# Sums of squares added on VectorE, two products with ones for sixteen, and the last tiles of mix by halves on VectorE

## The reference, cut to what matters

```
h = rms_norm(x, norm_mix_g);  proj = h @ w_in              # first norm
x = x + (gates0 * (o_a @ w_o[:512]) + gates1 * (o_b @ w_o[512:])) @ w_merge   # mix, merge
h = rms_norm(x, norm_ffn_g)                                # second norm
x = x + (silu(conv(h @ w_gate)) * (h @ w_up)) @ w_down     # feed-forward
# rms_norm(t, g) = t * rsqrt(mean(t*t) + 1e-6) * g
```

## Time and profile before

| | |
|---|---|
| median of 3 runs | 3369.89 us (3364.22 to 3376.41) |
| profiled execution | 3384.76 us, its span 3382.9 us |
| TensorE busy, span | 3193.5 us, 94% |
| VectorE | 2035.6 us, 60% |
| ScalarE | 1068.7 us, 32% |
| GpSimd | 315.4 us, 9% |
| granted clock, mean | 0.971 |

### The profile page before, as it was taken

How to read it: one execution, slowest core, us unless ns; L and a number is a source line. 1 busy time by engine, 2 the same in 40 slices (tenths; PEclk the granted TensorE clock), 3 DMA queues, 4 the chain that set the end, 5 groups by cost and what they waited for, 6 DMA issues and landing times.

```text
span 3382.9 us, 52078 instructions
## 1 busy us (share of the span) xinstructions
PE 3193.5 (94%) x22004; PEld 2545.1 (75%) x22004; DVE 2035.6 (60%) x3235; ACT 1068.7 (32%) x1526; POOL 315.4 (9%) x307
## 2 busy tenths in 40 slices
PE   8999998788988888999999999999998999999999
PEld 7777786576766767778888888877746888778887
DVE  4665454577777775534544444448979987655445
ACT  5222334444444442221111111122153333433332
POOL 0222342000000000401000000000000000000000
PEclk9999999789999998999999999999999999999999
DMA  3342666234344433421111111111101222213222
GB/s 143 118 137 68 220 209 202 62 83 100 83 105 98 95 66 136 149 93 38 50 50 50 50 50 44 44 38 42 46 13 50 99 89 99 87 69 129 90 99 75
DMA packets 93527, 301.86 MB, mean 89 GB/s; under 512 B 10352, under 2 KB 38640, under 8 KB 70768
## 3 DMA queue, kind: packets, MB, share of 16 engines
q1 hardware_dynamic: 79104, 246.63, 23.5%
q0 software_dynamic: 14192, 51.91, 4.5%
HBM read 241.35 MB, written 57.15 MB: 88 GB/s over the span
## 4 chain that ended last, share of the span: by engine, by line
PE 78%; DVE 11%; issue 3%; ACT 3%; DMA 3%; POOL 2%; SPq 1%; DVEq 0%; ACTq 0%; POOLq 0%
PE ps L2414 24%; PE ps L308 20%; PE ps L503 6%; PE ps L1755 3%; PE ps L2239 2%; PE ps L2556 2%; PE ps L1766 1%; PE ps L2074 1%; PE ps L1778 1%; PE ps L475 1%; DVE Yh L2583 1%; PE ps L1423 1%; PE ps L1019 1%; DMA Dn<-nbs 1%; PE ps L2434 1%
## 5 line engine op out<-in xcount | busy, mean ns | idle before, releaser
L2414 PE MATMUL ps<-Hh,whi 128*128 128x512 f32 x1600 | 498.4, 393 | 0.0
L284 ACT ACTIVATE whi<-raw 128x2048 fp32r<-128x2048 f32 x139 | 265.7, 1911 | 638.3 <-PE ps L308 310.4
L288 DVE TENSOR_TENSOR wlo<-raw,whi 128x2048 fp32r<-128x2048 f32 x139 | 319.0, 2295 | 132.9 <-ACT whi L284 132.7
L2414 PEld LDWEIGHTS ps<-Hh,whi 128*128 128x128 f32 x1600 | 300.5, 188 | 68.0 <-issue 6.2
L2414 PE MATMUL ps<-Hh,wlo 128*128 128x512 f32 x800 | 311.6, 390 | 0.0
L2414 PE MATMUL ps<-aHh,whi 128*128 128x512 f32 x512 | 200.0, 391 | 3.6 <-DVE xT L2760 2.5
L308 PE MATMUL ps<-Hhi,wlo 128*128 128x512 f32 x656 | 202.2, 389 | 0.0
L308 PE MATMUL ps<-Hhi,whi 128*128 128x512 f32 x656 | 202.1, 389 | 0.0
L308 PE MATMUL ps<-Hlo,whi 128*128 128x512 f32 x656 | 202.1, 389 | 0.0
L2414 PE MATMUL ps<-aHh,wlo 128*128 128x512 f32 x512 | 199.4, 389 | 0.0
L2414 PE MATMUL ps<-aLh,whi 128*128 128x512 f32 x512 | 199.4, 389 | 0.0
(11 more groups left out here) (385 smaller groups left out, 6199.9 us busy)
## 6 DMA issues: line engine op xcount, KB each, us to landing
raw<-in_panels SPq DMA_DIRECT2D x139, 1024.0 KB, 4.7
rwf<-F POOLq DMA_DIRECT2D x16, 1280.0 KB, 6.8
L<-rwf SPq DMA_DIRECT2D x16, 1024.0 KB, 5.0
L<-rwf SPq DMA_DIRECT2D x64, 256.0 KB, 4.1
Dn<-nbs SPq DMA_DIRECT2D x128, 128.0 KB, 5.4
gts<-so POOLq DMA_DIRECT2D x16, 512.0 KB, 3.2
gl<-gts SPq DMA_DIRECT2D x32, 256.0 KB, 3.6
rwt<-so POOLq DMA_DIRECT2D x15, 512.0 KB, 3.0
```

Of the source, the lines that this page charges most:

```text
L284: e.activation(whi[i % 2][:, :], raw_of(i)[:, :], AF.Copy).then_inc(*a_hi.up(i))
L288: e.tensor_tensor(wlo[i % 2][:, :], raw_of(i)[:, :], whi[i % 2][:, :].bitcast(F32), OP.subtract).then_inc(*v_lo.up(i))
L2414: m = e.matmul(ap, W[wi][:, kc, n0:n0 + 128], mov[mi][:, kc, :], start=x == 0 and q == 0, stop=x == len(kcs) - 1 and q == 2)
```

## The change

Squares are now added on VectorE (`acc_dve`: chunk 1's to chunk 0's in `rs`, and so on), and TensorE multiplies only the result by ones (`norm_pe`). ACT's square waits for the addition two chunks before. In the first norm the two products stand in the first half of mla1, before chunk 4; the wait for bank tiles in `rw_pe` follows the turned ring. In the second norm the squares and additions of chunks 0 to 6 (additions 1 to 6) go into merge, those of chunk 7 behind it, and the two products before chunk 3 of `together_pe`, which now does two outputs; gate 1 becomes a group of its own behind it. In merge VectorE drains an odd tile before it makes the next panel's low part. In mix, the additions of tiles 6 and 7 are VectorE's, half by half; ACT makes their `Hhi` by halves, and VectorE `Hlo`, with tile 6's beside tile 7. The diff, without what only moves the first norm's start into helpers:

```diff
@@ -319,8 +319,10 @@
             aps.append(ap)
         return aps
 
-    def together_pe(e, outs, mov, r, sig):
+    def together_pe(e, outs, mov, r, sig, third=None):
         for kc in range(8):
+            if kc == 3 and third:
+                third()
             e.wait_ge(*v_h.by(r, "lo", kc))
             for aps, w, n0, n1, key in outs:
                 for q, (wi, mi) in enumerate(THREE):
@@ -332,21 +334,28 @@
 
     a_h, v_h, t_h = signals("a_h"), signals("v_h"), signals("t_h")
 
-    def rms_act(e, r, gname, tmp, rs, x_by, h_free):
-        e.wait_ge(*d_vec.by())
-        for kc in range(8):
-            e.wait_ge(*x_by(kc))
-            if kc >= 2:
-                e.wait_ge(*t_h.by(r, "sum", kc - 2))
-            e.activation(tmp[kc % 2], xT[:, kc, :], AF.Square).then_inc(*a_h.up(r, "sq", kc))
-            if kc == 0:
-                for w in h_free:
-                    e.wait_ge(*w)
-            e.activation(Hhi[:, kc, :], xT[:, kc, :], AF.Copy, scale=vec(gname, kc)).then_inc(*a_h.up(r, "hi", kc))
+    def square_act(e, r, kc, tmp):
+        if kc >= 2:
+            e.wait_ge(*v_h.by(r, "acc", max(kc - 2, 1)))
+        e.activation(tmp[kc % 2], xT[:, kc, :], AF.Square).then_inc(*a_h.up(r, "sq", kc))
+
+    def hi_act(e, r, kc, gname):
+        e.activation(Hhi[:, kc, :], xT[:, kc, :], AF.Copy, scale=vec(gname, kc)).then_inc(*a_h.up(r, "hi", kc))
+
+    def sqrt_act(e, r, rs):
         e.wait_ge(*v_h.by(r, "mean", 1))
         e.activation(rs, rs, AF.Sqrt).then_inc(*a_h.up(r, "sqrt"))
 
-    def rms_pe(e, r, tmp):
+    def acc_dve(e, r, kc, tmp, rs):
+
+        e.wait_ge(*a_h.by(r, "sq", kc))
+        if kc == 1:
+            e.tensor_tensor(rs, tmp[0], tmp[1], OP.add).then_inc(*v_h.up(r, "acc", kc))
+        else:
+            e.wait_ge(*v_h.by(r, "acc", kc - 1))
+            e.tensor_tensor(rs, rs, tmp[kc % 2], OP.add).then_inc(*v_h.up(r, "acc", kc))
+
+    def norm_pe(e, r, rs):
         aps = []
         for h in range(2):
             ap, waits = ring.take(("sum", r, h), (v_h, r, "mean", h))
@@ -354,25 +363,22 @@
                 e.wait_ge(*w)
             aps.append(ap)
         e.wait_ge(*d_cc.by())
-        for kc in range(8):
-            e.wait_ge(*a_h.by(r, "sq", kc))
-            for h in range(2):
-                m = e.matmul(aps[h], ones, tmp[kc % 2][:, hs(h)], start=kc == 0, stop=kc == 7)
-            m.then_inc(*t_h.up(r, "sum", kc))
-
-    def rms_dve(e, r, gname, rs, rs_free=()):
-        e.wait_ge(*d_vec.by())
-        for kc in range(8):
-            e.wait_ge(*a_h.by(r, "hi", kc))
-            e.scalar_tensor_tensor(out=Hlo[:, kc, :], in0=xT[:, kc, :], scalar=vec(gname, kc),
-                                   in1=Hhi[:, kc, :].bitcast(F32), op0=OP.mult,
-                                   op1=OP.subtract).then_inc(*v_h.up(r, "lo", kc))
-        e.wait_ge(*t_h.by(r, "sum", 7))
-        for w in rs_free:
-            e.wait_ge(*w)
+        e.wait_ge(*v_h.by(r, "acc", 7))
+        for h in range(2):
+            e.matmul(aps[h], ones, rs[:, hs(h)], start=True, stop=True).then_inc(*t_h.up(r, "sum", h))
+
+    def h_lo_dve(e, r, kc, gname):
+        e.wait_ge(*a_h.by(r, "hi", kc))
+        e.scalar_tensor_tensor(out=Hlo[:, kc, :], in0=xT[:, kc, :], scalar=vec(gname, kc), in1=Hhi[:, kc, :].bitcast(F32),
+                               op0=OP.mult, op1=OP.subtract).then_inc(*v_h.up(r, "lo", kc))
+
+    def means_dve(e, r, rs):
+        e.wait_ge(*t_h.by(r, "sum", 1))
         for h in range(2):
             e.tensor_scalar(rs[:, hs(h)], ring.bank("sum", r, h), 1.0 / KB, 1e-6, OP.mult,
                             OP.add).then_inc(*v_h.up(r, "mean", h))
+
+    def over_dve(e, r, rs):
         e.wait_ge(*a_h.by(r, "sqrt"))
         e.reciprocal(rs, rs).then_inc(*v_h.up(r, "rs"))
...
         e.wait_ge(*d_vec.by())
@@ -470,6 +457,8 @@
                 for kc in range(8):
                     if i == 0 and js[0] == 0:
                         e.wait_ge(*v_h.by(0, "lo", kc))
+                    if i == 1 and js[0] == 0 and kc == 4:
+                        norm_pe(e, 0, rs)
                     for j in js:
                         for q, (mi, wi) in enumerate(((0, 0), (0, 1), (1, 0))):
                             m = e.matmul(aps[j][:, 0:208], H2[mi][:, kc, 128 * j:128 * (j + 1)], W[wi][:, kc, :],
@@ -477,8 +466,6 @@
                         if kc == 7:
                             m.then_inc(*t_mla.up(i, j))
             last_use[p] = (t_mla, (i, 7))
-            if i == 0:
-                rms_pe(e, 0, tmp)
 
     def mla_act(e, i, j):
         e.wait_ge(*t_mla.by(i, j))
@@ -519,7 +506,7 @@
             if n0 == 0:
                 panel_pe(e, p)
             if ch < 2:
-                e.wait_ge(*a_mla.by("cols", 1, 6 * ch + 1))
+                e.wait_ge(*a_mla.by("cols", 1, 4 * ch + 3))
             front_pair(e, ("rw", ch), v_rw, "u", ch)
         half_group(e, [fring.bank("rw", ch, h) for h in range(2)], W, n0, n0 + M, half, t_rw, ch)
         if half:
@@ -1972,7 +1959,7 @@
             e.wait_ge(*(v_mx if h else g_mx).by("m", n - 1, h))
         e.dma_start(gl0[y % 2], gts[n][:, hs(h)]).then_inc(*d_g0.up(y))
         if y >= 3:
-            e.wait_ge(*g_mx.by(*seq[y - 3]))
+            e.wait_ge(*added(*seq[y - 3]))
         if y == 2:
             e.wait_ge(*t_mx.by("OT", 3, 0))
         e.dma_start(gl1[y % 3], gts[8 + n][:, hs(h)]).then_inc(*d_g1.up(y))
@@ -2124,8 +2111,13 @@
             if n == 4:
                 panel_act(e, WO + 4)
             e.wait_ge(*v_mx.by("OA", 3))
-            e.wait_ge(*g_mx.by(n, 1))
-            e.activation(Hhi[:, n, :], mix[n][:, :], AF.Copy).then_inc(*a_h.up("mix", "hi", n))
+            if n < 6:
+                e.wait_ge(*added(n, 1))
+                e.activation(Hhi[:, n, :], mix[n][:, :], AF.Copy).then_inc(*a_h.up("mix", "hi", n, 1))
+            else:
+                for h in range(2):
+                    e.wait_ge(*added(n, h))
+                    e.activation(Hhi[:, n, hs(h)], mix[n][:, hs(h)], AF.Copy).then_inc(*a_h.up("mix", "hi", n, h))
         panel_act(e, WO + 5)
 
     def mix_dve(e):
@@ -2144,21 +2136,35 @@
                 e.wait_ge(*d_g1.by(2 * n + h))
                 e.tensor_tensor(gl1[(2 * n + h) % 3], ring.bank("yb", n, h), gl1[(2 * n + h) % 3],
                                 OP.mult).then_inc(*v_mx.up("b", n, h))
-            if n:
+                if n >= 6:
+                    e.wait_ge(*(v_mx if h else g_mx).by("m", n, h))
+                    e.wait_ge(*v_mx.by("b", n, h))
+                    e.tensor_tensor(mix[n][:, hs(h)], mix[n][:, hs(h)], gl1[(2 * n + h) % 3], OP.add).then_inc(*v_mx.up("sum", n, h))
+                if n == 7:
+                    mixlo_dve(e, 6, h)
+            if 1 <= n < 7:
                 mixlo_dve(e, n - 1)
-        mixlo_dve(e, 7)
+        for h in range(2):
+            mixlo_dve(e, 7, h)
         panel_dve(e, WO + 5)
 
-    def mixlo_dve(e, n):
-        e.wait_ge(*a_h.by("mix", "hi", n))
-        e.tensor_tensor(Hlo[:, n, :], mix[n][:, :], Hhi[:, n, :].bitcast(F32), OP.subtract).then_inc(*v_h.up("mix", "lo", n))
+    def added(n, h):
+
+        return v_mx.by("sum", n, h) if n >= 6 else g_mx.by(n, h)
+
+    def mixlo_dve(e, n, h=None):
+        t = slice(0, S) if h is None else hs(h)
+        e.wait_ge(*a_h.by("mix", "hi", n, 1 if h is None else h))
+        m = e.tensor_tensor(Hlo[:, n, t], mix[n][:, t], Hhi[:, n, t].bitcast(F32), OP.subtract)
+        if h != 0:
+            m.then_inc(*v_h.up("mix", "lo", n))
 
     def mix_pool(e):
         for n in range(8):
             e.wait_ge(*a_mx.by("ya", n, 0))
             e.wait_ge(*d_g0.by(2 * n))
             e.tensor_tensor(mix[n][:, hs(0)], mix[n][:, hs(0)], gl0[0], OP.mult).then_inc(*g_mx.up("m", n, 0))
-            for h in range(2):
+            for h in range(2 if n < 6 else 0):
                 if h:
                     e.wait_ge(*v_mx.by("m", n, 1))
                 else:
@@ -2244,16 +2250,36 @@
 
     def merge_dve(e):
         for n in range(8):
-            if n % 2:
-                panels_after(panel_dve, e, UIX[f"mg{n // 2}"])
             e.wait_ge(*d_xs.by(n))
             for h in range(2):
                 e.wait_ge(*t_mg.by(n, h))
                 e.tensor_tensor(xT[:, n, hs(h)], ring.bank("mg", n, h), xs[n % 2][:, hs(h)], OP.add).then_inc(*v_mg.up(n, h))
+            if n in (1, 3, 5):
+                panels_after(panel_dve, e, UIX[f"mg{n // 2}"])
+            if 1 <= n < 7:
+                acc_dve(e, 1, n, tmp2, rs2)
+        h_lo_dve(e, 1, 0, "norm_ffn_g")
+        acc_dve(e, 1, 7, tmp2, rs2)
+        for kc in range(1, 8):
+            h_lo_dve(e, 1, kc, "norm_ffn_g")
+        means_dve(e, 1, rs2)
+        panels_after(panel_dve, e, UIX["mg3"])
+        over_dve(e, 1, rs2)
 
     def merge_act(e):
-        for n in range(1, 8, 2):
-            panels_after(panel_act, e, UIX[f"mg{n // 2}"])
+        for n in range(7):
+            e.wait_ge(*v_mg.by(n, 1))
+            square_act(e, 1, n, tmp2)
```

(57 more changed lines are left out.)

## The result

The changed kernel takes 3350.2 us in the median of 6 runs (3346.2 to 3356.4), beside 3371.93 (3364.22 to 3377.88) of the kernel before in 6. The ratio is 0.9937, 95% interval [0.9922, 0.9953]: 21 us shorter (16 to 26 by the interval), and 3350.7 had been forecast. The profiled execution took 3347.74.

What follows compares the result with a forecast made beforehand. The prediction took TensorE, with 78% of the chain of waits, to bound the kernel. First norm 5.9, mix 0 and second norm 13.3 summed to 19.2 us, so 3350.7 us against the median of 3369.89; its own range was 3344 to 3357.

Steps and rivals of the forecast that it cites:

- First norm, TensorE's side: First norm's products with ones: 11.7 us go, 1.7 stay; TensorE pauses 1.1 us for the last addition at 46.2.
- The root moves less: First norm's root and rst come only 2.7 us earlier; TensorE pauses 1.5 us more for tile copies.
- Latents: ACT's lat squares wait for rst instead of tile copies, so they and VectorE's latent work come 7.4 us earlier.
- ckv pause and half rate: TensorE's wait for ckv grows to 4.0 us; 7.4 passes, less 1.5 for a half-rate stretch: 5.9 us gained.
- Mix: Mix's last tiles, additions moved from POOL to VectorE: 0 us, bounds -1.5 (gain) and +2.8.
- Second norm: Between merge and feed-forward: 15.94 gone, 1.7 and 1.4 back, 0.5 pause gained: 13.3 us, bounds 11.5 and 15.
- Sum: Whole kernel: 5.9 + 0 + 13.3 = 19.2 us, giving 3350.7 against the median of 3369.89.
- Rival 1: Both norms' products pass in full, 23.4 us, plus the pause's 0.5: 3346 us; chance 0.14.
- Rival 2: Only the second norm pays, the first gives 2.7 or less: 16 us, 3354; chance 0.22 together with Rival 3.
- Rival 3: Additions don't overlap other work; first norm's TensorE gain is 0: 13 us, 3357; chance 0.22 together with Rival 2.
- Rival 4: Front part: TensorE pauses at each latent handover, then half rate; 20 stretches give 3380.7, 11 us slower; chance 0.04.

Runs made afterwards that it cites:

- no_mix: The changed kernel with mix's part undone; ratio to the kernel before 0.9934.
- warm_tail: The changed kernel plus 22 unread products issued while TensorE waits for mix's tile 6; ratio to the kernel before 0.9926.
- norm1_alone: The kernel before with only the first norm's part of the change; ratio to the kernel before 0.9954.
- early_norm: The changed kernel with the second norm's high and low parts of chunks 0 to 2 made during merge's last tile; ratio to the kernel before 0.9895.
- norm2_alone: The kernel before with only the second norm's part of the change; ratio to the kernel before 0.9958.
- mix_alone: The kernel before with only mix's part (tiles 6 and 7 added on VectorE, in halves); ratio to the kernel before 0.9994.
- root_late: The changed kernel with the first norm's two products before chunk 7 instead of chunk 4; ratio to the kernel before 0.9947.
- alone_products: The changed kernel with the first norm's two products between the two projections, where sixteen stood; ratio to the kernel before 0.9942.
- latents_first: The changed kernel with VectorE's rope of the shared key behind the ckv pieces instead of ahead; ratio to the kernel before 0.9903.

## Why the prediction was right

By its own steps:

- **First norm, TensorE's side.** Pause 1.1 foretold, 1.34 measured; last addition at 46.2, was 46.83. Additions take 1.31 us each (7.87 for six), not 1.26, and the projection began 0.5 later.
- **The root moves less.** 2.7 foretold, 53.32 - 51.39 = 1.9 measured. The tile copies' pause was 0.95, not 1.5.
- **Latents.** 7.4 earlier foretold, 74.44 - 67.80 = 6.6 measured: the same mechanism (ACT waited for rst, 1.85 us), shifted by the 0.8 us by which the root came later than I had it.
- **ckv pause and half rate.** A pause of 4.0 us was foretold, a gain of 7.4 at ckv, and one more stretch at half rate, so 5.9. Measured are 4.47, 7.1 counted from ACT's first copy, and 5.9 by the means at the front's end. That the last number is met to the tenth is luck, as two things behind ckv show that the prediction did not have. First, half rate: the kernel before has a stretch behind its pause of 2.44 us at 130.84. Changed, no_mix and warm_tail have one behind ckv and none behind that later pause, so in them it moved rather than came. norm1_alone and early_norm have both, as foretold (rows below). Second, TensorE waits for a DMA (`lw`) at 338 to 347 us, 5.29 and 4.92 us in the kernel before's profiles, 3.76 and 4.04 in norm2_alone and mix_alone, and 3.54 to 4.33 in the five with the change. Both scatter from profile to profile, so the 7.4 us between the first pair is one draw, and the mean is the better measure of the term.
- **Mix.** 0 foretold; merge's stretch is 1.8 us longer in the pair of profiles, 0.9 by means, and nothing with y_a in front of it. Chunk 6 came as described: 0.8 us later was foretold, and it came 4.74 instead of 3.95 behind the last gate tile. The pauses grew by 0.4 us together; the rest is the half rate, which lasted longer than the 3.4 us that I had carried over from the earlier trace rows.
- **Second norm.** 13.3 foretold, 13.4 measured, and its steps held: pause 2.6 (2.65), half rate behind it, chunk 3 unheld, root in time (2.2 us to spare, 3 foretold).
- **Sum.** 5.9 + 13.4 = 19.3 by stages where the means are used, with nothing or 0.9 off for mix; 19.2 foretold, 21.7 by medians, 16 to 26 by the interval.

```profile
126.78 0.73 PE L784 MATMUL ps<-ukv_hi,ckv 128*128 128x512 f32 x2 [2.44 <-DVE XN L840]
...
127.84 1.05 PE L784 MATMUL ps<-ukv_hi,ckv 128*128 128x512 f32 x2
```

These are TensorE's rows in early_norm, at the pause that the changed kernel has at 125.63.

Against the span of the first profile, the changed one is 37 us shorter: 7.4 in the front, 13.1 in the scan, 3.6 in y_a, 13.4 in norm 2, 1.2 in the rest, less 1.8 in merge. Had the sum been read off two profiles, it would have seemed off by a factor of two.

Three pauses, two new (0.95 and 1.34 us) and one grown from 2.28 to 4.47, brought one stretch of half rate in the first norm, so the sum with one such stretch was the nearer one. The Trainium skill, TensorE: Matmul & The Clock Gate, section "What's actually happening", has the half rate as the default that activity lifts; by that rule each of the three could have cost 1.5 us, and the trace agrees for one of them.

Rival 1 fell with root_late and norm1_alone, since not all of the products' 11.7 us passed (7.1 at ckv). Rival 2 fell with the same 7.1 and with a front 5.9 us shorter by means, where it had 2.7 or less. Rival 3 fell with additions that ended at 46.83. Rival 4 fell since VectorE's other handovers in the front keep TensorE's pauses (4.47, 2.86 and 3.45 against 4.47, 2.86 and 3.47), and since at most one stretch at half rate came on top, where 13 were needed.

## What to carry to other kernels

Work taken from the engine that bounds is worth what the next wait leaves of it: follow the value that it makes (here the root, then rst, latents, ckv) to the first instruction that the bounding engine issues on it. Laying a short product beside other products can be the whole gain, and removing products none of it, as alone_products shows; and an operand prepared as soon as its last reader is through, chunk by chunk, removes the pause between two stages (4.5 us with the half rate behind it). Cut profiles into stages before subtracting them, count each event from a near one (to ckv, the same code repeated within 0.1 us, to the front's end within 3), and take several profiles of a stage whose clock varies: one stage can scatter by more than the change is worth.

## What the runs showed of the hardware

- Pauses of equal length (2.65 us) at the same place were followed by half rate in one execution (changed) and by full rate in another (latents_first); a pause of 2.44 likewise, with the same front's code (half rate in early_norm, none in the changed kernel).
- A stretch at half rate lasted 2.7 us behind merge (from 1480.32 to the pair at 1483.02) and 5.3 behind mix (1395.73 to 1401.02) in one profile.
- Unread products keep the rate: 22 of them, 5.15 us, made merge 3.2 us shorter (93.6 against 96.8).
- The scan, the same instructions on the same data, took 739.0 and 742.6 us in one kernel's two profiles and 724.6 to 737.4 in others, with the clock between 0.90 and 0.93 and VectorE and ACT equally busy (within 1 us).
